# Two groups of turned probabilities on ScalarE, the newest unit's exponents behind them, and masks first in the accumulators

## What is computed

```python
logits = jnp.einsum('bshd,bnhd->bhsn', q, k).astype(jnp.float32) * (HEAD_DIM ** -0.5)
logits = jnp.where(valid, logits, -jnp.inf)      # A: selected keys; C: causal; memory: all keys
p = jax.nn.softmax(logits, axis=-1).astype(v.dtype)
out = jnp.einsum('bhsn,bnhd->bshd', p, v)
```

## Time and profile before

| | us |
|---|---|
| runs: median (lowest to highest) of 3 | 1568.5 (1567.89 to 1568.8) |
| the profiled execution, own time | 1570.32 |
| its span, from first to last instruction | 1568.5 |
| TensorE busy in it | 1540.1 (98%) |
| VectorE busy | 1082.9 (69%) |
| ScalarE busy | 747.5 (48%) |
| mean granted clock of TensorE | 0.996 of full |

### The profile page before, as it was taken

The page is one execution under the profiler, slowest core; times in us unless marked ns, Lnnn a source line. Parts: engine busy times, 40 slices in busy tenths (PEclk is TensorE's granted clock), DMA queues, the critical chain, the costliest instruction groups (busy, mean ns, idle before and its releaser), DMA issues. The chain is left out here.

```text
span 1568.5 us, 19812 instructions
## 1 busy us (share of the span) xinstructions
PE 1540.1 (98%) x8189; PEld 1276.4 (81%) x8189; DVE 1082.9 (69%) x1387; ACT 747.5 (48%) x933; POOL 52.3 (3%) x89
## 2 busy tenths in 40 slices
PE   8999999999999999999999999999999999999997
PEld 6887788888878888888788888877888887978986
DVE  5885957747677776576866756877766678567764
ACT  5545544443444444345544343555444434474463
POOL 1100000000000000000000000000100000000010
PEclk9999999999999999999999999999999999999999
DMA  7752466654425766452466654523775546424530
GB/s 281 268 212 81 175 241 240 251 206 178 172 81 178 291 240 247 157 194 102 175 237 246 242 222 148 201 108 105 271 269 223 217 168 240 155 107 155 210 126 27
DMA packets 45898, 299.87 MB, mean 191 GB/s; under 512 B 5540, under 2 KB 5796, under 8 KB 12528
## 3 DMA queue, kind: packets, MB, share of 16 engines
q1 hardware_dynamic: 39168, 277.96, 47.5%
q0 software_dynamic: 5776, 19.01, 3.9%
q10 hardware_dynamic: 864, 1.64, 0.3%
HBM read 296.20 MB, written 2.65 MB: 191 GB/s over the span
## 5 line engine op out<-in xcount | busy, mean ns | idle before, releaser
L1707 DVE TENSOR_TENSOR w_low<-w_raw,w_high 128x2048 fp32r<-128x2048 f32 (+1 forms) x240 | 543.9, 2271 | 36.9 <-ACT w_high L1479 35.5
L1479 ACT ACTIVATE w_high<-w_raw 128x2048 fp32r<-128x2048 f32 (+1 forms) x240 | 456.8, 1904 | 228.0 <-DMA w_raw<-in_weights 141.2
L1107 PE MATMUL psum<-w_high,xt_high 128*128 128x512 f32 (+1 forms) x1408 | 554.2, 394 | 7.8 <-DVE w_low L1703 3.9
L1109 PE MATMUL psum<-w_high,xt_low 128*128 128x512 f32 (+1 forms) x1408 | 543.9, 386 | 0.0
L1108 PE MATMUL psum<-w_low,xt_high 128*128 128x512 f32 (+1 forms) x1408 | 543.5, 386 | 0.0
L1107 PEld LDWEIGHTS psum<-w_high,xt_high 128*128 128x128 f32 x1408 | 265.1, 188 | 64.6 <-DVE w_low L1703 5.3
L1109 PEld LDWEIGHTS psum<-w_high,xt_low 128*128 128x128 f32 x1408 | 265.0, 188 | 54.1
L1108 PEld LDWEIGHTS psum<-w_low,xt_high 128*128 128x128 f32 x1408 | 265.4, 188 | 49.5
L2028 DVE TENSOR_TENSOR arena<-arena,psum 128x256 f32<-128x256 f32 x88 | 37.0, 420 | 204.2 <-ACT arena L1601 203.8
L1107 PE MATMUL psum<-w_high,ht_high 128*128 128x512 f32 x352 | 140.8, 400 | 0.0
L1601 ACT ACTIVATE arena<-psum 128x256 f32<-128x256 f32 x88 | 33.7, 383 | 218.3 <-PE psum L1109 218.3
(11 more groups left out here) (243 smaller groups left out, 1500.6 us busy)
## 6 DMA issues: line engine op xcount, KB each, us to landing
w_raw<-in_weights SPq DMA_DIRECT2D x260, 1024.0 KB, 4.8
norm_params<-in_ln_g POOLq DMA_DIRECT2D x8, 512.0 KB, 4.4
norm_params<-in_ln_b POOLq DMA_DIRECT2D x8, 512.0 KB, 5.8
w_raw<-in_weights SPq DMA_DIRECT2D x4, 656.0 KB, 6.1
kv_outside<-arena POOLq DMA_DIRECT2D x3, 512.0 KB, 4.9
mem_kv<-kv_outside POOLq DMA_DIRECT2D x3, 512.0 KB, 3.6
norm_params<-mods_outside POOLq DMA_DIRECT2D x3, 512.0 KB, 6.0
w_raw<-in_weights SPq DMA_DIRECT2D x4, 256.0 KB, 9.3
```

Of the source, the lines that this page charges most:

```text
L1107: e.matmul(dst, a_hi, b_hi, start=first, stop=False)
L1109: return e.matmul(dst, a_lo, b_hi, start=False, stop=last)
L1479: e.activation(K.w_hi[:, g % RING, 0:w], K.w_raw[:, r, 0:w], ACT.Copy).then_inc(K.high.hit(t), 1)
L1707: e.tensor_tensor(K.w_lo[:, s, 0:w], K.w_raw[:, r, 0:w], K.w_hi[:, s, 0:w].bitcast(F32), ALU.subtract).then_inc(K.taken.hit(t), 1)
```

## The change

- `group_on_scalar` takes the group too. It is true for both groups of every unit that isn't dilated, so that ScalarE copies both. Dilated units have at most four pieces, and VectorE goes on copying them.
- In `unit`, the exponents of units that aren't dilated move from the second step to the third, just ahead of the reciprocal. In an iteration the list then reads: the new unit's scores, the oldest's weighing, the middle's turns, the new's exponents and reciprocal.
- In TensorE's `scores`, masks that cover all of a unit's keys are issued ahead of the products of queries and keys, and not behind them. Dilated units and the causal mask over 128 of 256 keys keep the old order.

```diff
@@ class Plan, unit
         if by_rows(job):
             self.add("exps", job)
         yield
+        yield
         if not by_rows(job):
             self.add("exps", job)
-        yield
-        if not by_rows(job):
             self.add("recip", job)
         yield
@@ tensor_program, scores
-        work += [(n, K.identb, b, b.shape[1]) for n, b in enumerate(bias)]
+        masks = [(n, K.identb, b, b.shape[1]) for n, b in enumerate(bias)]
+        work = work + masks if j.kind == "dil" or bias and bias[0].shape[1] < nk else masks + work
@@ scalar_program, turn_prob
-        if g != K.group_on_scalar(j):
+        if not K.group_on_scalar(j, g):
             return
@@ vector_program, turn_prob
-        if g == K.group_on_scalar(j):
+        if K.group_on_scalar(j, g):
             return
@@ class Kernel
-    def group_on_scalar(self, j):
+    def group_on_scalar(self, j, g):
 
-        return None if self.unit_pieces(j) <= 4 else 0 if by_rows(j) else 1
+        return g == 0 and self.unit_pieces(j) > 4 if by_rows(j) else True
```

## The result

The changed kernel takes **1577.0 us** (median of 6 runs, 1576.4 to 1577.7) against 1568.2 (6 runs, 1567.1 to 1570.7): ratio **1.0056**, 95% interval 1.0044 to 1.0067, or 8.8 us more. The forecast was 1578.0, in a range of 1571.5 to 1583.

A forecast was written before the change was run, and what follows sets the result against it. The prediction took TensorE, busy in 98% of the span, as the bound, so only its waits count. Chains +7.0 and clock +2.5 gave +9.5 on 1570.32, 1579.8, less 1.8 for the median: 1578.0, range 1571.5 to 1583.

The forecast's parts named there:

- The copy itself: Moving 23 group 0 copies from VectorE to ScalarE: 15.6 us off VectorE, none on the path, so 0.
- Exponents 1.35 later: In an ordinary attention iteration, exponents queue behind both copies and start 1.3 to 1.4 us later.
- First unit: First units of layers 0 and 3: exponents behind an evacuation, first turn waits for normalised probabilities, +1.3 us each.
- Values late: Layer 0's fourth iteration: weighing waits for the late evacuation of the values' second row block, +0.6 us; layer 3 +0.75.
- End chain: Last iterations of a layer: serial chain through exponents, normalising, rounding rest and maximum, +1.4 us in layer 0, +1.45 in layer 3.
- Layer 2: Its 1.42 us wait for values grows by 0.9; with the chain's share at the seventh iteration, +1.4 us.
- Masks: Masks issued first in twelve units: bounded by 1.4 us either way, taken as 0.
- The clock: Falls from 2.4 to 1.2 GHz near the ends of layers 0 and 3, +1.1 and +1.4: +2.5 us.
- Chain without clock: Rival: only the chains' +7.0 us, 1575.5; chance 0.22, shared with the case of one fall.
- Relief: Rival: VectorE without its copies reaches later work earlier and TensorE's waits go, -4.0 us, 1564.5; chance 0.06.
- Hidden: Rival: unseen slack takes up the chains and removed waits balance the rest, no change, 1567 to 1570; chance 0.12.
- Clock worse: Rival: a fall lasts twice as long or comes in layer 2 too, +1.7 to 3.4 more, 1580 to 1583; chance 0.10.

The follow-up runs named there:

- e2: Kernel before with only the exponents moved behind the turns, VectorE still copying group 0: 1578.1 us against 1567.3, ratio 1.0062.
- e3: Kernel before with both groups' copies on ScalarE, exponents left in their old place: 1569.7 us against 1567.3, ratio 1.0010.
- e5: Kernel before with only the first unit's exponents of layers 0 and 3 put one step later: 1570.8 us against 1568.0, ratio 1.0018.
- e4: Changed kernel with the first unit's exponents of layers 0 and 3 back in their old place: 1574.7 us, ratio to before 1.0046.
- e7: Changed kernel with the evacuation of the values' second row block moved from VectorE to ScalarE: 1573.6 us, ratio to before 1.0036.
- e11: Changed kernel executed once more, nothing edited, to see whether the slow clock keeps its places: 1576.7 us.
- e9: Changed kernel with the edits of e4 and e7 together: 1572.1 us against 1568.2 before, ratio 1.0023.
- e1: Kernel before with only the masks moved ahead of the products of queries and keys: 1567.6 us against 1567.3, ratio 1.0002.
- e8: Changed kernel with 16 extra matmuls inside each of TensorE's two long waits in layers 2 and 3: 1577.0 us, ratio to before 1.0058.
- e10: Kernel before with e6's edit, the last memory unit's exponents later in layers 0, 2, 3, and a rounding rest ahead of them: 1564.0 us against 1568.2.
- e6: Kernel before with the evacuation of the values' second row block moved from VectorE to ScalarE: 1568.0 us against 1568.0, ratio 0.9999.

## Why the prediction was right, step by step

**The copy itself, 0.** Right for the copy as the change places it: e2 has the whole loss without it. Without the reordering it costs about 2 us (e3, 1.0010), where it stands behind the exponents and pushes ScalarE's later work.

**Exponents 1.35 later.** Right: 1.34 in the trace. The working held because it went by when the second turn can be read, not by the lengths of two copies.

**First unit, 1.3 each.** Mis-sized by 0.2: 1.52 and 1.53. The trace of layer 0 shows two small terms that the sum lacked. Counted from the start of the first iteration in either trace, L1985 starts 2.47 later than before, and not 2.2 to 2.3. And turns restart 1.10 us after the start of L1985 rather than 0.96, since TensorE's wait ends about 0.14 behind the end of VectorE's row. e5 adds the part alone, 2.8 us by the medians, and e4 takes it away.

**Values late, 0.6.** Right (0.67), and e7 shows the cause. Layer 3's appears as forecast only in executions without the fall ahead of it (0.73 in e11, forecast 0.75).

**End chain, 1.4 for layer 0, 1.45 for layer 3.** Right in size, 1.36 and 1.32, and e9 has it with the other parts mended, though one wait was missing from the account: the product behind the sixth iteration stands 0.81 us for its rest, so part of the loss comes one iteration sooner.

**Layer 2, 1.4.** Nearly right without the clock: in e2, where no fall stands in layer 2, the layer adds 1.1 (2.79 to 3.90). With its fall it adds 2.0.

**Masks, 0.** Right, e1.

**The clock, 2.5.** This is the step that failed in its parts. I had put falls at the ends of layers 0 and 3 and taken away the one of layer 3's third iteration. The profiled execution has them in layer 2's fifth and, still, in layer 3's third. The forecast had two new falls at +2.5 and one gone at -1.05 (the 7.0 of the chains holds that relief, so the rival *Chain without clock* wasn't quite without it): +1.45 for the clock and 8.05 for the chains alone. Measured is one more fall than before, 1.6 at its place and about 0.8 net (e8), and no relief. Taking 0.8 from the table's 8.8 leaves 8.0 for the chains, an estimate from these two traces and e8. Over all traces of the changed kernel and its variants the fall is found at any of four places (about 174, 753, 1060 and 1089), and in e10 at a fifth, each time behind a stretch of waits, and the same program shows two or one of them. So its price could be bounded from the rows, but its place could not be named. That the sum, 9.5, is so near to 8.8 is in this term luck: a fall expected in one place came in another.

**The rivals.** *Relief* falls with e3, slower by about 2 and not faster. Its point of decision was the right one to look at: e10 wins just where VectorE waited for the sums, by giving it other work there and not by taking copies from it. *Hidden* falls with the result. *Chain without clock* (1575.5) is near the lowest of the changed kernel's runs, 1576.4, but none goes that low. *Clock worse* has its fall in layer 2, but not its price, since the two at the ends of layers 0 and 3 didn't come; by its own terms that price ends at 1578.0 + 3.4 = 1581.4, and 1583 needs the masks' 1.4 as well.

## What to carry to other kernels

In an engine that works in order, an early place for a short instruction is paid by everything behind it, and the price is set by when its input is ready (here the second transpose), not by its own length: moving four exponents of 0.47 us behind the copies made them 1.34 us later in each ordinary iteration, which cost nothing while there was slack and 8.8 us in all, clock included, where it had run out. Follow a late result on through the next engine's queue to the first wait of the bound engine, and count it there; a wait that goes may uncover the next (e6), so measure mends together as well as alone. Where an engine idles for a result and owes work that is needed later, put that work into the hole (e10).

## What the runs showed of the hardware

The granted clock falls from 2.4 to 1.2 GHz (a mean of 0.57 over the 4 us window that holds the fall) behind waits of TensorE: one of 1.5 to 2.3 us in attention at 753, 759 and 1060 (1054 before), three of 0.60, 0.46 and 1.03 us in e4 at 174. Whether it does at a given place differs between executions of one program: 753 and 1060 us in one, 752 alone in the other. What TensorE did ahead of the place doesn't tell them apart here:

```profile
1056.00:1060.00 4.00, 1.80 (x22) 1.20 (x19) 1.73 (x3) 2.31 (x9) 0.00 (x0) 1.00 0.55 233
1056.30:1060.30 4.00, 1.77 (x21) 1.18 (x20) 1.78 (x3) 2.31 (x9) 0.00 (x0) 1.00 0.53 219
169.60:173.60 4.00, 1.92 (x21) 1.21 (x15) 4.00 (x4) 3.30 (x5) 0.00 (x0) 1.00 0.16 64
170.00:174.00 4.00, 1.91 (x15) 1.20 (x12) 4.00 (x4) 3.08 (x4) 0.00 (x0) 1.00 0.09 33
```

The first two are the changed kernel (a fall follows) and e11 (none), the last two the changed kernel (none) and e4 (a fall). The same stretch had a fall in e7 and e8 too. The runs of one kernel spread by 1 to 6 us, which is as much as several of the edits measured here, and the faster ones show the higher mean clock in most sets (e3 above; in e4 0.997 at 1572.8 and 1573.6, 0.994 at 1575.4 and 1577.9). What decides where the clock falls I can't say from these runs.
